# Who waits for the join: the packing copy on ScalarE or the transposing transfer on SyncE

## The reference, cut to what matters

```python
proj = rmsnorm(x) @ w_in          # split into a_b, a_c, a_x, a_z, c_q, c_kv, k_pe, b_z, dq, dk, dv, c_z, gates
u = a_c * a_x                     # branch a: causal convolution of 3 taps
y_a = a_b * conv(u) * silu(a_z)
y_b = causal_attention(q, k, v) * silu(b_z)             # branch b: 8 heads, low-rank q and kv
y_c = dilated_attention(rms(dq), rms(dk), dv) * silu(c_z)  # branch c: 3 dilations, 8 heads, one softmax over all
merged = g_a * (y_a @ w_out_a) + g_b * (y_b @ w_out_b) + g_c * (y_c @ w_out_c)
x = x + merged @ w_o
```

## Time and profile before

| what | value |
|---|---|
| median of 3 runs | 1267.4 us (1266.32 to 1268.23) |
| the profiled execution, its own time | 1267.36 us |
| its span, first to last instruction | 1265.5 us |
| PE busy | 1258.6 us (99% of the span) |
| DVE busy | 921.0 us (73%) |
| ACT busy | 786.1 us (62%) |
| POOL busy | 100.3 us (8%) |
| granted TensorE clock | 1.000 |

### The profile page before, as it was taken

One profiled execution on the slowest core, in us unless ns is written; L12 is line 12 of the kernel. 1 busy time (PEld: TensorE's weight loads), 2 busy tenths in 40 slices (PEclk: granted clock), 3 DMA queues, 4 the chain that ended last, 5 costly groups with the idle time before them and its releaser, 6 DMA issues.

```text
span 1265.5 us, 17020 instructions
## 1 busy us (share of the span) xinstructions
PE 1258.6 (99%) x6644; PEld 1049.3 (83%) x6644; DVE 921.0 (73%) x1056; ACT 786.1 (62%) x1018; POOL 100.3 (8%) x77
## 2 busy tenths in 40 slices
PE   9999999999999999999999999999999999999999
PEld 7888888987778888888888887888888889878887
DVE  6576556687987865556678787985867878798675
ACT  6676545568755666655685976464457778656541
POOL 0000000000000100000146000000012630000000
PEclk9999999999999999999999999999999999999999
DMA  9786637532466776663677778675657686667662
GB/s 348 237 290 226 221 103 251 172 125 83 150 217 218 240 231 204 214 227 127 175 231 186 218 226 221 171 254 187 206 174 248 189 216 217 211 173 218 214 199 84
DMA packets 152641, 256.39 MB, mean 203 GB/s; under 512 B 95344, under 2 KB 95472, under 8 KB 152432
## 3 DMA queue, kind: packets, MB, share of 16 engines
q1 hardware_dynamic: 149680, 246.45, 61.8%
q10 hardware_dynamic: 2880, 8.84, 2.3%
HBM read 232.19 MB, written 1.05 MB: 184 GB/s over the span
## 4 chain that ended last, share of the span: by engine, by line
PE 83%; DVE 6%; ACT 3%; POOL 3%; issue 2%; DMA 2%; SPq 0%; ACTq 0%; another core or an unknown queue 0%; POOLq 0%; DVEq 0%
PE psum L2147 24%; PE psum L2168 23%; PE psum L2148 23%; PE psum L2153 2%; PE psum L2200 2%; PE psum L2154 2%; PE psum L2346 2%; DMA raw<-weights 2%; DVE w_lo L1338 2%; PE psum L2215 2%; POOL rstd L643 2%; POOL mean L639 1%; PE psum L2600 1%; ACT w_hi L699 1%; ACT planes L1146 1%
## 5 line engine op out<-in xcount | busy, mean ns | idle before, releaser
L1338 DVE TENSOR_TENSOR w_lo<-raw,w_hi 128x1024 fp32r<-128x1024 f32 x219 | 265.1, 1222 | 127.0 <-ACT w_hi L699 125.7
L699 ACT ACTIVATE w_hi<-raw 128x1024 fp32r<-128x1024 f32 x219 | 228.6, 1055 | 114.9 <-PE psum L2168 77.8
L2147 PE MATMUL psum<-w_hi,x_hi 128*128 128x512 f32 (+1 forms) x632 | 248.8, 394 | 0.4 <-ACT w_hi L699 0.4
L2148 PE MATMUL psum<-w_hi,x_lo 128*128 128x512 f32 (+1 forms) x632 | 245.8, 389 | 0.0
L1338 DVE TENSOR_TENSOR y_lo<-raw,y_hi 128x1024 fp32r<-128x1024 f32 x139 | 168.6, 1221 | 48.1 <-ACT y_hi L699 47.2
L2168 PE MATMUL psum<-w_lo,x_hi 128*128 128x512 f32 (+1 forms) x632 | 194.7, 389 | 0.0
L699 ACT ACTIVATE y_hi<-raw 128x1024 fp32r<-128x1024 f32 x139 | 145.8, 1056 | 64.7 <-PE psum L2168 30.9
L2147 PE MATMUL psum<-y_hi,x_hi 128*128 128x512 f32 (+1 forms) x424 | 166.4, 393 | 0.0
L2148 PE MATMUL psum<-y_hi,x_lo 128*128 128x512 f32 (+1 forms) x424 | 165.0, 389 | 0.0
L2147 PEld LDWEIGHTS psum<-w_hi,x_hi 128*128 128x128 f32 x632 | 118.9, 188 | 27.2 <-issue 3.0
L2168 PEld LDWEIGHTS psum<-w_lo,x_hi 128*128 128x128 f32 x632 | 118.7, 188 | 24.9 <-DVE w_lo L1338 0.4
(11 more groups left out here) (230 smaller groups left out, 2039.9 us busy)
## 6 DMA issues: line engine op xcount, KB each, us to landing
raw<-weights SPq DMA_DIRECT2D x406, 512.0 KB, 4.3
probs<-weights SPq DMA_DIRECT2D x8, 512.0 KB, 5.6
probs_t<-weights SPq DMA_DIRECT2D x8, 512.0 KB, 5.5
arena<-gains ACTq DMA_DIRECT2D x7, 512.0 KB, 4.4
arena<-gate_bias ACTq DMA_DIRECT2D x6, 512.0 KB, 4.2
norm<-x_feat SPq DMA_DIRECT2D x4, 256.0 KB, 5.0
res<-x SPq DMA_DIRECT2D x2, 512.0 KB, 8.4
arena<-lru_w ACTq DMA_DIRECT2D x1, 1024.0 KB, 4.9
```

The source lines that it names most:

```text
L699: act.activation(slot(t)[0], raw_place(t), ACT.Copy).then_inc(hi_ready, 1)
L1338: dve.tensor_tensor(lo, raw_place(t), hi.bitcast(F32), ALU.subtract).then_inc(lo_ready, 1)
L2147: pe.matmul(out_, l_hi, r_hi, start=start, stop=False, skip_group_check=skip)
L2148: pe.matmul(out_, l_lo, r_hi, start=False, stop=False, skip_group_check=skip)
```

## The change

Two places change. On SP, a transfer waits for the join of the job ahead only if it is one of the two row jobs of a layer. On ACT, a row job's pack waits for the transfer of the job ahead as before; any other job's pack waits for the join of the job ahead.

```diff
+        ROWS_SWAPS = [rows_job(n, l) for l in range(LAYERS) for n in range(ROWS)]
...
                 if t in LAYER_SWAPS:
                     sp.wait_ge(planes_packed, LAYER_SWAPS[t])
-                    if LAYER_SWAPS[t] > 1:
+                    if LAYER_SWAPS[t] in ROWS_SWAPS:
                         sp.wait_ge(planes_joined, LAYER_SWAPS[t] - 1)
                     sp.dma_start_transpose(swapped.rearrange("p (b s) -> p b s", s=P), planes[:, :]
...
-                def planes_free(count):
+                def planes_pack(count, words):
 
-                    if count > 1:
+                    if count in ROWS_SWAPS:
                         act.wait_ge(planes_swapped, 16 * (count - 1))
-
-                def planes_pack(count, words):
-
-                    planes_free(count)
+                    elif count > 1:
+                        act.wait_ge(planes_joined, count - 1)
                     act.activation(by_plane(planes), by_word(words.bitcast(U16)), ACT.Copy).then_inc(planes_packed, 1)
```

## The result

The changed kernel takes **1270.6 us** (median of 10 runs, 1268.72 to 1272.8) and the kernel before 1267.59 us (10 runs, 1266.08 to 1268.38) on the same chip: 1.0024 [1.0015, 1.0034] of the time before. That is 3.0 us or 0.24% slower, with 1.0000 outside the interval, and about as forecast (1271.2 us). The trace shows that the forecast number is a sum of other terms than those I had written down.

What follows compares the result with a forecast made beforehand. PE was taken as the bound, busy 1258.6 of 1265.5 us. The terms 0 + 0 + 1.90 + 1.95 = 3.85 us on 1267.36 gave 1271.2 us, range 1268.8 to 1273.2.

Steps and rivals of the forecast that it cites:

- Part 1: SP's wait for the join goes for 30 transfers: expected 0, at most a gain of 0.9 us.
- Part 2: Later packs of dilated jobs 2 and 3 on ACT: lag dies in idle time, expected 0.
- Rival 2: The dilated stage costs too, its lag reaching PE: up to 1.6 us more, 1272.8 us; chance 14%.
- Part 3: Unit 5's pack behind the first row job's join delays line 749's copies: DVE lags 1.35 us a layer.
- Part 4: Unit 7's pack behind the second row job's join delays a refill: DVE's lag grows from 1.35 to 1.95 us.
- Rival 1: Not slower: DVE's lag in the units is lost before it reaches PE, 1268.5 or 1267.4 us; chance 18%.
- Rival 3: Hardly anything is hidden: all four delays of each layer reach PE, 18.7 us, 1286 us; chance 3%.
- Rival 4: Faster or no change: SP's waits cost more than shown, 0.9 us gain giving 1266.5 us; chance 3%.
- the granted clock stays at 1.000: Sign expected in the changed kernel's profile: no fall of the granted clock.

Runs made afterwards that it cites:

- Experiment 3: Kernel before, with SP's wait for the join taken out for nine jobs of each layer, packs untouched: 1267.98 us, ratio 0.9999.
- the first trace: Profiled execution of the changed kernel, the slowest of its ten runs: own time 1272.8 us.
- experiment 1: Kernel before, with only dilated jobs 2 and 3 of both layers packing behind the join ahead: 1265.03 us, ratio 0.9979.
- experiment 9: Changed kernel with the two copies of line 749 put ahead of unit 5's pack on ACT: 1265.92 us, 0.9988 of the kernel before.
- the second trace: The unaltered changed kernel run once more; the traced execution is its fastest, 1268.75 us, median 1270.03 us.
- experiment 4: Kernel before plus two DVE waits a layer for POOL's first instruction of dilated jobs 3 and 4, no job moved: 1265.17 us, ratio 0.9979.
- experiment 10: Kernel before plus one DVE wait a layer, ahead of line 2078, for POOL's first instruction of dilated job 3: 1265.08 us, ratio 0.9981.
- experiment 5: Kernel before, with only unit 5 of both layers packing behind the first row job's join: 1271.4 us, ratio 1.0034.
- experiment 2: Kernel before, with only units 5 and 7 of both layers packing behind the join of the row job ahead: 1272.15 us, ratio 1.0035.

## Why the prediction was right in its number and wrong in a term

**Part 1, SP: right.** Experiment 3 moved the time by 0.9999 [0.9990, 1.0008]. The rule of dependency chains, weighed there, has no gain to show here. The transfers that lost their wait are 29 and not 30, as the very first job had none; the page's count of instructions fell from 17020 to 16991.

**Part 2, "Dilated jobs 2 and 3, expected 0": wrong, and this is the step that failed.** The delays of the packs were as worked out, and no lag was left behind the stage. But I followed job 2's lag on ACT alone and missed that its late refill stops DVE too. And I read the 2.22 us of DVE's idle time ahead of 675.48, marked "issue", as room, and did not ask what ended it. It was POOL's reciprocal root, which ended at 675.39, late because the instruction ahead of it had been kept out for 4.71 us. With the late refill POOL gets in earlier, and DVE gets these 2.22 us back. The bounds of the sum had no gain for this part, and no reason for leaving it out. By the marks the gain is 1.5 and 1.2 us in the two layers of the first trace and 1.6 and 0.9 us in the second; experiment 1 alone gains 2.9 us. Rival 2 (this stage costs) fell with it.
The Trainium skill (SBUF — State Buffer, Summary: rules for kernel authors) has the rule that I should have weighed: where a DVE instruction has two SBUF inputs while GpSimd's reads SBUF, "the second one to issue **fully blocks** until the first finishes". For dilated job 1 the trace of before agrees: POOL's instruction ends 0.05 us after the DVE instruction that it met. For jobs 3 and 4 it was held beyond the sentence, not by the DVE instruction that it met but also by those behind it: 4.58 us from line 1338 to line 1546.

**Part 3, unit 5: mechanism right, its price too low.** The copies of line 749 are the way (experiment 9), and the second trace has the 1.35 us in it. But alone the move cost 3.8 us, not 2.6. The prediction added nothing for a later landing of the row transfer (1.5 us in one layer), for a refill that waits for its weight load (0.7 us in one layer) or for the clock (1.7 us); each stands in a trace, but not in every one.

**Part 4, unit 7: right.** 0.54 us of wait for the refill, 1.1 us for the move alone against 1.2, and 2.0 us a layer for both units against 1.90 and 1.95. Rivals 1, 3 and 4 fell: the lag reached PE, the four delays did not all do so, and the wait on SP gave nothing.

**The sum.** I wrote 0 + 0 + 1.90 + 1.95 = 3.85. The fast trace holds -1.6 + 2.0 - 0.9 + 2.0 = 1.5 us. The slow one has 4.8 instead of 2.0 us in the first layer's units, with two things that I had taken as constant: the second row transfer's landing, 1.7 us later, and the clock, 1.7 us ("the granted clock stays at 1.000" failed in it). The median lies between them, 3.0 us above before. So the gain that I left out (2.5 us in the fast trace) was made up for by costs that I left out, 3.0 - 3.85 + 2.5 = 1.7 us at the median. That 1271.2 us was hit within 0.6 us is luck.

**Better than both.** Experiments 1, 4 and 10 all stand at 1265.0 to 1265.2 us, 0.2% under the kernel before. The cheapest is experiment 10, one wait on DVE per layer, with no change to the order of packs and joins. Whether it adds to the reordered copies of experiment 9 was not tried.

## What to carry to other kernels

Idle time of an engine is only room for a delay if one knows what ends it: follow each idle stretch to the instruction that ends it, above all one marked "issue", and where it is a tiny instruction with a long duration, ask what kept that out. Moving a pack later helped here by accident, and the same gain was had on purpose by a wait that lets the small engine go first. Price a new wait by the instructions queued behind the waiting one, and look whether they can be put ahead of it; that took away the cost here without undoing the change.

## What the runs showed of the hardware

- One POOL instruction on 128x16 floats (dilated jobs 3 and 4) took 4.58 to 5.03 us beside DVE instructions that followed each other without a stop, and 0.20 to 2.18 us where DVE had been made to wait for 0.09 to 0.77 us nearby. Elsewhere (632.28 us in the kernel before) it took 1.03 us beside DVE instructions that overlap just so; what decides is open. The reciprocal root behind it took 2.90 to 3.89 us.
- The granted clock fell to the lower of its two levels for 3.4 us behind waits of PE's weight loads of 2.37, 2.43 and 2.44 us, once in each of three traces. Behind waits of 2.02, 2.07 and 2.13 us it stayed at 1.000, and behind the longest of all, 2.46 us in experiment 5, too. So the length of the wait alone does not decide; what does is open. Four runs with a listed clock under 1.000 in the changed kernel's eighteen are between 1271.16 and 1272.8 us.
- The transfer of the second row job landed 5.2 to 5.4 us after its issue in the first layer of the first trace of the change and of experiment 5, and 3.6 to 3.8 us after it in their second layers and in both layers of the other twelve traces. The same kind of transfer took 3.6 to 7.6 us over the 34 jobs of the kernel before. Why these two were late stays open; a packet of an instruction queue lies near the transfer in slow and in quick cases alike. So does why the weight load behind unit 7's pack came late in the second layer of experiments 2 and 5.
